# Compressed attention scores computed with the keys stationary and turned back by a stacked identity, and another order of products in attention's tail

## The chip, the cores and the metric

The kernel runs on one core of a Trainium2 chip. Times are device microseconds (us) of one execution. The kernel before took 708.16 us (median of 3 runs, 706.64 to 710.5). The change is judged by the same figure for the kernel after. The engines are named as in the profile: PE is TensorE (PEld its weight load), DVE VectorE, ACT ScalarE, POOL GpSimd, SP the queue that issues the weight loads.

## What is computed

A trunk of two equal layers over 256 tokens of width 1024. Each layer projects x, runs a short gated convolution on one half of the width and sparse attention (8 query heads in 2 key groups) on the other, normalises each head, projects back, adds and normalises; then comes a gated feed-forward part. The change touches one of attention's three branches, the compressed one, and what stands around it:

```python
sub = a.reshape(B, G, nsub, CMP_STRIDE, dk)
blocks = jnp.concatenate([sub[:, :, j:j + nc] for j in range(r)], axis=3)
k_cmp = gelu(blocks @ w1 + b1) @ w2 + b2          # nc = 15 compressed keys in each of 2 groups
sc = jnp.einsum('bgrqd,bgcd->bgrqc', qc, k_cmp)   # the compressed scores
p_cmp = _masked_softmax(sc, cmp_end[None, :] <= t[:, None])
o_cmp = jnp.einsum('bgrqc,bgcd->bgrqd', p_cmp, v_cmp)
out = g0 * o_cmp + g1 * o_slc + g2 * o_win
mixed = _head_rmsnorm(jnp.concatenate([conv_out, attn_out], -1), head_norm_g[i])
x = _layer_norm(ALPHA * x + mixed @ w_out[i], ln1_g[i], ln1_b[i])
```

## The kernel before

Everything is one program with the order on each engine written out by hand; the engines meet only at semaphores. The weights come through SP as units of 128x2048 numbers into three `raw` buffers. ACT rounds a unit to `ring_hi` (`split_hi`), DVE forms the remainder `ring_lo` (`split_lo`), and only then can the raw buffer be loaded again and PE use the unit. A precise product is three matmuls (`mm3`, L1194 to L1196): high by high, high by low, low by high. Plain float32 matmuls, such as those of L1279, L1345 and L1358, stand in the profile as two instructions each.

Attention is a loop over 12 blocks n = 0 to 11 (eight of 256 query-key columns for two heads, four of 128 columns for four heads). PE does, for each n: `scores(n+2)`, `transpose_p(n+1)` (L1266), some quarters of the convolution's projection (`conv_unit`), and `times_v(n)` (L1279). DVE takes the maxima and copies the transposed probabilities to `probsT` (L870); ACT takes the exponentials (`exps(n)`, L502). ACT works its list in order, and between `exps(n)` and `exps(n+1)` it does what the table `between` names: roundings of weights, parts of the convolution.

In the pass n = 10 PE also does, one after the other: the first product of the output projection (`out_part(L, 0, 0, 0)`, six matmuls of 512 columns, one mm3 for each half of the width), `mean_squares(L, 1)` (L1358: eight instructions of 2 columns), and `cmp_scores`, in which the queries are stationary and the 30 compressed keys `kcTh`, `kcTl` move: 2 token tiles by 4 head pairs by 3 matmuls, 24 matmuls of 30 columns. What follows is called the tail here: the last two `times_v`; `out_part(L, 0, 0, 1)`; `transpose_cmp` (L1336), which waits for the compressed softmax on DVE and ACT; `conv_roots(L, 1)` (L1368), which waits for a chain `copy_squares` (DVE L924), roots (POOL L704, L706), `roots_high` (ACT L510), `roots_low` (DVE L929); `times_v_cmp` for both token tiles (L1345); `out_part(L, 1, 0, 0)` and `(L, 1, 0, 1)`, which write banks 0 and 1; `out_unit(L, 0, 1)`; `heads_T(L, 0)` (L1388), six more matmuls, `heads_T(L, 1)`, and the rest of the output projection. Between `times_v_cmp` and `heads_T` lies a chain over three engines: DVE adds the compressed output (L910), ACT squares it, DVE sums (L915), POOL takes the root (L706), DVE scales (L920).

The first layer normalisation begins on DVE with `residual` (L952), after the splits of units 19 and 20, the first two of the feed-forward part.

## Time and profile before

| what | value |
|---|---|
| median of 3 runs | 708.16 us |
| the profiled execution | 708.14 us |
| its span, first to last instruction | 706.2 us |
| PE busy | 689.5 us, 98% |
| DVE busy | 519.5 us, 74% |
| ACT busy | 370.0 us, 52% |
| mean granted TensorE clock | 0.983 |

The profiled execution is the median one to 0.02 us, and 1.94 us of it lie outside its span. Busy time is no time at full speed: a matmul at half the clock is as busy as one at the full clock and takes up to twice as long. So for PE the row of the granted clock is read beside the busy share.

### The profile page before, as it was taken

To read this page: it belongs to the slowest core of one execution; us is meant where nothing else is said; L and a number is where in the kernel's file an instruction comes from. 1 tells how busy PE (TensorE), PEld (TensorE's weight loads), DVE (VectorE), ACT (ScalarE), POOL (GpSimd) and SP (SyncE) were. 2 spreads that over 40 slices of the span, in tenths; PEclk is the share of its full clock that TensorE was granted. 3 is DMA by queue.
4 is the path that set the end of the run, shared out by engine and by line. 5 is a ranking of instruction groups with operands and counts; after the bars stand their busy time and mean duration, and the time that the engine had idled before them with its cause. 6 is when DMAs were issued, how large, how long until landed. Compare 5 with 4: busy or idle time off the path is not lost.

```text
span 706.2 us, 11208 instructions
## 1 busy us (share of the span) xinstructions
PE 689.5 (98%) x4310; PEld 604.1 (86%) x4310; DVE 519.5 (74%) x762; ACT 370.0 (52%) x556; POOL 95.4 (14%) x54
## 2 busy tenths in 40 slices
PE   8999999999999999999999999999999999999995
PEld 5899998877998888888878999988889888888884
DVE  4675768768897777777696466697859977777756
ACT  5664535423776555666356443553248666666630
POOL 0000020221262111110000000204005511111000
PEclk9999999699999999999999999998999999999999
DMA  9971443332765555555338233513357855555301
GB/s 294 318 253 62 151 148 120 120 100 80 261 239 192 195 196 195 197 201 185 122 120 267 91 120 120 176 65 120 120 183 235 294 182 178 179 178 178 119 0 59
DMA packets 87401, 116.81 MB, mean 165 GB/s; under 512 B 5230, under 2 KB 73536, under 8 KB 87360
## 3 DMA queue, kind: packets, MB, share of 16 engines
q1 hardware_dynamic: 85920, 111.85, 47.6%
q10 hardware_dynamic: 1440, 4.39, 1.9%
q8 instruction: 28, 0.46, 0.3%
q14 instruction: 13, 0.11, 0.0%
HBM read 115.19 MB, written 1.05 MB: 165 GB/s over the span
## 4 chain that ended last, share of the span: by engine, by line
PE 92%; DVE 5%; DMA 1%; issue 1%; ACT 1%; SPq 0%; DVEq 0%; ACTq 0%
PE bank L1194 19%; PE bank L1196 18%; PE bank L1195 18%; PE bank L1454 17%; PE bank L1456 9%; PE bank L1279 3%; PE bank L1266 2%; DMA x_tok<-in_x 1%; PE bank L1215 1%; DVE x_tok L970 1%; DVE stats L954 1%; DVE x_tok L952 1%; PE bank L1258 1%; PE bank L1345 1%; DVE ring_lo L308 1%; DVE x_tok L978 1%
## 5 line engine op out<-in xcount | busy, mean ns | idle before, releaser
L308 DVE TENSOR_TENSOR ring_lo<-raw,ring_hi 128x2048 fp32r<-128x2048 f32 x102 | 232.6, 2285 | 23.0 <-ACT ring_hi L304 22.7
L304 ACT ACTIVATE ring_hi<-raw 128x2048 fp32r<-128x2048 f32 x102 | 194.3, 1908 | 13.2 <-DMA raw<-in_w_in 9.3
L1454 PE MATMUL bank<-xx,ring_hi 128*128 128x512 f32 x512 | 181.4, 398 | 0.0
L1456 PE MATMUL bank<-xx,ring_lo 128*128 128x256 f32 x512 | 143.8, 281 | 0.0
L1454 PEld LDWEIGHTS bank<-xx,ring_hi 128*128 128x128 f32 x512 | 96.2, 188 | 23.8
L1456 PEld LDWEIGHTS bank<-xx,ring_lo 128*128 128x128 f32 x512 | 96.7, 189 | 0.6
L721 POOL COPY step_par<-ffn_par 128x16 f32 (+1 forms) x22 | 64.3, 2927 | 221.5 <-DVE work L989 221.5
L1194 PE MATMUL bank<-xx,ring_hi 128*128 128x256 f32 x320 | 92.4, 289 | 0.0
L1195 PE MATMUL bank<-xx,ring_hi 128*128 128x256 f32 x320 | 90.5, 283 | 0.0
L1196 PE MATMUL bank<-xx,ring_lo 128*128 128x256 f32 x320 | 90.5, 283 | 0.0
L1194 PE MATMUL bank<-ring_hi,xx 128*128 128x512 f32 (+1 forms) x224 | 81.5, 364 | 3.8 <-DVE xx L783 3.8
L989 DVE SCALAR_TENSOR_TENSOR work<-conv_o,step_par,work 128x254 f32<-128x254 f32 (+1 forms) x128 | 56.2, 480 | 38.4 <-ACT work L560 37.2
L1194 PE MATMUL bank<-ring_hi,hTh 128*128 128x512 f32 (+1 forms) x224 | 81.0, 362 | 0.0
L1196 PE MATMUL bank<-ring_hi,hTl 128*128 128x512 f32 (+1 forms) x224 | 80.3, 358 | 0.0
L1195 PE MATMUL bank<-ring_lo,hTh 128*128 128x512 f32 (+1 forms) x224 | 80.1, 358 | 0.0
L1196 PE MATMUL bank<-ring_hi,xx 128*128 128x512 f32 (+1 forms) x224 | 78.1, 349 | 0.0
L1195 PE MATMUL bank<-ring_lo,xx 128*128 128x512 f32 (+1 forms) x224 | 77.9, 348 | 0.0
L556 ACT ACTIVATE conv_o<-bank 128x256 f32<-128x256 f32 x64 | 24.3, 379 | 74.1 <-PE bank L1456 74.1
L1194 PEld LDWEIGHTS bank<-xx,ring_hi 128*128 128x128 f32 x320 | 61.3, 192 | 0.2
L1195 PEld LDWEIGHTS bank<-xx,ring_hi 128*128 128x128 f32 x320 | 61.4, 192 | 0.0
L1196 PEld LDWEIGHTS bank<-xx,ring_lo 128*128 128x128 f32 x320 | 61.3, 192 | 0.0
L1194 PEld LDWEIGHTS bank<-ring_hi,xx 128*128 128x128 f32 x224 | 43.1, 192 | 11.2 <-DVE xx L783 3.8
(186 smaller groups left out, 998.1 us busy)
## 6 DMA issues: line engine op xcount, KB each, us to landing
raw<-in_w_up SPq DMA_DIRECT2D x44, 1024.0 KB, 5.2
raw<-in_w_down SPq DMA_DIRECT2D x22, 1024.0 KB, 5.0
raw<-in_w_in SPq DMA_DIRECT2D x21, 1024.0 KB, 5.2
raw<-in_cmp_w SPq DMA_DIRECT2D x8, 1024.0 KB, 5.9
raw<-in_w_out SPq DMA_DIRECT2D x8, 1024.0 KB, 4.8
qkv<-in_ln_g ACTq DMA_DIRECT2D x4, 512.0 KB, 3.6
qkv<-in_ln_b ACTq DMA_DIRECT2D x4, 512.0 KB, 5.0
raw<-in_w_in SPq DMA_DIRECT2D x2, 512.0 KB, 5.1
```

The costliest lines, as they stand in the source:

```text
L304: nc.scalar.activation(ring_hi[slot_of(L, u)][:], raw[raw_of(L, u)][:], ACT.Copy).then_inc(hi_done, 1)
L308: eng.tensor_tensor(ring_lo[slot_of(L, u)][:], raw[raw_of(L, u)][:], ring_hi[slot_of(L, u)][:].bitcast(fp32), ALU.subtract).then_inc(split ...
L556: nc.scalar.activation(up_y[:, 2 * v + c, :], bank[JOINED_BANK[2 * v + c]][:, SEQ:2 * SEQ], ACT.Copy).then_inc(up_low, 1)
L721: nc.gpsimd.tensor_copy(step_par[:, odd].rearrange("p v c k -> p (v c k)"), ffn_par[:, bass.ds(s, 1)].rearrange("p o v c k -> p (o v c k)"))\
L989: ins = V.scalar_tensor_tensor(ffn_y[:, odd, v, c, back:], up_source(s, odd, v, c)[:, 0:SEQ - back], step_par[:, odd, v, c, 2 - back:3 - b ...
L1194: pe.matmul(dst, ah, bh, start=start, stop=False, **kw)
L1195: pe.matmul(dst, ah, bl, start=False, stop=False, **kw)
L1196: return pe.matmul(dst, al, bh, start=False, stop=stop, **kw)
L1266: ins = pe.transpose(bank[6 + n % 2][:, P * m:P * (m + 1)], probs[n % 2][:, P * m:P * (m + 1)], ident)
L1279: ins = pe.matmul(bank[2][:, HEAD * (NPAIR * g + h):HEAD * (NPAIR * g + h + 1)], probsT[n % 2][:, P * (kb * j + b):P * (kb * j + b + 1)], ...
L1454: pe.matmul(dst[:], wh[:, k, P * c:P * (c + 1)], xx[:, k].rearrange("p a n -> p (a n)"), start=k == 0, stop=False)
L1456: ins = pe.matmul(dst[:, 0:SEQ], wl[:, k, P * c:P * (c + 1)], xh[:, k, :], start=False, stop=k == KT - 1)
```

## The change

The two key tiles become one, `kcT`, with high and low keys side by side (2 x 30 columns). `cmp_scores_wide(L, m)` makes them stationary and moves the queries of two head pairs, 2 x 256 columns, past them: one matmul gives 60 rows (high keys and low keys by high queries), a second adds high keys by low queries to the first 30 rows. It runs at the ends of the passes n = 4 and n = 6, into bank 3. ACT copies the 60 x 512 result to `cmp_sT` (`copy_wide`), once after `conv_init` behind `exps(5)`, once after `roots_high` behind `exps(7)`. In the pass n = 10 `cmp_scores` then only turns the result back: eight plain float32 matmuls with a 60 x 128 piece of `cmp_sT` stationary and an identity stacked twice (60 x 30, 30 more columns of the constants) moving, which also adds the two halves.

In the tail the order changes: the first product is divided around `mean_squares`, `out_part(L, 0, 0, 1)` moves ahead of `times_v(10)`, `conv_roots(L, 1)` and the two parts of token tile 1 move ahead of `transpose_cmp`, whose waits for the banks become weaker (the subtraction of the maxima instead of the exponentials). On DVE the split of unit 19 moves from before `copy_pT(11)` to between the two groups of `mix_low`.

```diff
+        kcT = sb("kcT", [P, 2, NG, NBLK], f32r)
+        kcTh, kcTl = kcT[:, 0], kcT[:, 1]
+        cmp_sT = sb("cmp_sT", [2 * NG * NBLK, 2, 2 * SEQ])
...
+            def copy_wide(L, m):
+                act.wait_ge(cmp_wide, 2 * L + m + 1)
+                nc.scalar.activation(cmp_sT[:, m, :], bank[3][0:2 * NG * NBLK, :], ACT.Copy).then_inc(cmp_wide_copied, 1)
...
-                           5: [lambda: conv_init(L, 1)], 6: [lambda: split_hi(act, L, 17)], 7: [lambda: roots_high(L, 0)],
+                           5: [lambda: conv_init(L, 1), lambda: copy_wide(L, 0)], 6: [lambda: split_hi(act, L, 17)],
+                           7: [lambda: roots_high(L, 0), lambda: copy_wide(L, 1)],
...
                 copy_squares(L, 1)
-                split_lo(V, L, 19)
                 copy_pT(L, 11)
...
                         mix_low(4 + j, xl[:, 4 + j, tok], xh[:, 4 + j, tok], bank[6 + t][:, P * j:P * (j + 1)])
-                split_lo(V, L, 20)
+                    split_lo(V, L, 19 + t)
...
+            def cmp_scores_wide(L, m):
+
+                if m == 0:
+                    pe.wait_ge(ms_read, 2 * L + 1)
+                    pe.wait_ge(cmp_copied, 2 * L + 2)
+                else:
+                    pe.wait_ge(cmp_wide_copied, 2 * L + 1)
+                n = NG * NBLK
+                heads = slice(2 * m, 2 * m + 2)
+                pe.matmul(bank[3][0:2 * n, :], kcT[:].rearrange("p a g c -> p (a g c)"),
+                          qTh[:, heads, :].rearrange("p i n -> p (i n)"), start=True, stop=False, skip_group_check=True)
+                pe.matmul(bank[3][0:n, :], kcTh.rearrange("p g c -> p (g c)"),
+                          qTl[:, heads, :].rearrange("p i n -> p (i n)"), start=False, stop=True,
+                          skip_group_check=True).then_inc(cmp_wide, 1)
+
             def cmp_scores(L):
...
-                        ins = mm3(bank[0][:, c0:c0 + NG * NBLK], qTh[:, h, tok], qTl[:, h, tok],
-                                  *(a[:].rearrange("p g c -> p (g c)") for a in (kcTh, kcTl)), True, True)
+                        col = SEQ * (h % 2) + P * t
+                        ins = pe.matmul(bank[0][:, c0:c0 + NG * NBLK], cmp_sT[:, h // 2, col:col + P],
+                                        cst[0:2 * NG * NBLK, C_ST:C_ST + NG * NBLK], start=True, stop=True)
...
                     elif n == 10:
                         pe.wait_ge(conv_out, 2 * L + 2)
-                        out_part(L, 0, 0, 0)
+                        wait_unit(L, U_OUT)
+                        wait_mix(L, 0, 0)
+                        out_product(L, 0, 0, 0)
                         mean_squares(L, 1)
+                        out_product(L, 0, 1, 0)
                         cmp_scores(L)
                     if n < 11:
                         transpose_p(L, n + 1)
+                    if n == 10:
+                        out_part(L, 0, 0, 1)
...
                     times_v(L, n)
-
-                out_part(L, 0, 0, 1)
+                    if n in (4, 6):
+                        cmp_scores_wide(L, (n - 4) // 2)
+
+                conv_roots(L, 1)
+                pe.wait_ge(exp_done, N_ATT * L + 12)
+                pe.wait_ge(max_done, N_ATT * L + 13)
+                out_part(L, 1, 0, 0)
+                out_part(L, 1, 0, 1)
                 transpose_cmp(L)
-                conv_roots(L, 1)
                 times_v_cmp(L, 0)
                 times_v_cmp(L, 1)
-                pe.wait_ge(exp_done, N_ATT * L + 13)
-                out_part(L, 1, 0, 0)
-                out_part(L, 1, 0, 1)
                 out_unit(L, 0, 1)
```

Three places in the order of instructions matter later. The first is ACT's list from `exps(5)` to `exps(8)`, the exponentials of four blocks with what lies between them. Before:

```order
L502 ACTIVATE probs,rsum<-bank,nmax 128x256 x2
L475 ACTIVATE conv_y<-conv_z,par 128x256 x2
L502 ACTIVATE probs,rsum<-bank,nmax 128x128 x4
L304 ACTIVATE ring_hi<-raw 128x2048
L502 ACTIVATE probs,rsum<-bank,nmax 128x128 x4
L510 ACTIVATE hTh<-croot 128x512
L502 ACTIVATE probs,rsum<-bank,nmax 128x256 x2
```

The same piece of the kernel after:

```order
L506 ACTIVATE probs,rsum<-bank,nmax 128x256 x2
L479 ACTIVATE conv_y<-conv_z,par 128x256 x2
L529 ACTIVATE cmp_sT<-bank 60x512
L506 ACTIVATE probs,rsum<-bank,nmax 128x128 x4
L308 ACTIVATE ring_hi<-raw 128x2048
L506 ACTIVATE probs,rsum<-bank,nmax 128x128 x4
L514 ACTIVATE hTh<-croot 128x512
L529 ACTIVATE cmp_sT<-bank 60x512
L506 ACTIVATE probs,rsum<-bank,nmax 128x256 x2
```

Each copy of a wide result now stands directly before the exponentials of a block, those of `exps(6)` and of `exps(8)`. The second place is PE at the end of the pass n = 4 of the kernel after, from `times_v(4)` to the first matmuls of `scores(7)`:

```order
L1287 MATMUL bank<-qkv,probsT 128x64 x4
L1337 MATMUL bank<-qTh,kcT 60x512
L1339 MATMUL bank<-qTl,kcT 30x512
L1202 MATMUL bank<-kTh,qTh 128x128
L1203 MATMUL bank<-kTl,qTh 128x128
L1204 MATMUL bank<-kTh,qTl 128x128
```

The two wide matmuls stand between `times_v(4)` and `scores(7)`, where nothing stood; at the end of the pass n = 6 it is the same with `scores(9)`. The third place is DVE's list from the scaling of the heads (`mroot`) to the first `residual`. Before, and then after:

```order
L920 TENSOR_TENSOR work<-work,mroot 128x512 x2
L938 SCALAR_TENSOR_TENSOR xx<-bank,par,xx 128x128 x8
L308 TENSOR_TENSOR ring_lo<-raw,ring_hi 128x2048
L952 SCALAR_TENSOR_TENSOR x_tok<-x_tok,bank 128x512
L954 BN_STATS stats<-x_tok 128x6
```

```order
L929 TENSOR_TENSOR work<-work,mroot 128x512 x2
L947 SCALAR_TENSOR_TENSOR xx<-bank,par,xx 128x128 x4
L312 TENSOR_TENSOR ring_lo<-raw,ring_hi 128x2048
L947 SCALAR_TENSOR_TENSOR xx<-bank,par,xx 128x128 x4
L312 TENSOR_TENSOR ring_lo<-raw,ring_hi 128x2048
L961 SCALAR_TENSOR_TENSOR x_tok<-x_tok,bank 128x512
```

A second split has moved in between the heads and the residual.

## Rows read from the trace of the kernel before

**Rows 1.** The page: granted TensorE clock in 40 slices of the span.

```profile
PEclk9999999699999999999999999998999999999999
```

**Rows 2.** Windows: stretch and length, busy us (instructions) of each engine, PEclk, DMA.

```profile
126.24:129.56 3.32, 3.32 (x31) 3.27 (x29) 3.31 (x3) 1.99 (x3) 1.12 (x1) 1.00 0.02 6
129.56:143.21 13.65, 13.65 (x46) 10.81 (x47) 8.57 (x22) 4.37 (x6) 2.70 (x2) 0.50 0.47 154
477.72:484.55 6.83, 6.83 (x29) 6.14 (x27) 5.97 (x18) 2.72 (x3) 1.97 (x2) 0.50 0.85 282
171.50:173.17 1.67, 0.00 (x0) 0.00 (x0) 0.75 (x2) 1.65 (x4) 0.00 (x0) 1.00 0.30 110
```

**Rows 3.** Timeline of PE, passes 4 to 7, layer 0: start, us, engine, line, operation.

```profile
105.33 1.00 PE L1279 MATMUL bank<-qkv,probsT 128*128 128x64 f32 x8
106.25 0.33 PE L1194 MATMUL bank<-kTh,qTh 64*128 64x128 f32 x1
...
107.96 0.60 PE L1266 MATMUL bank<-cst,probs 128*128 128x128 f32 x4
...
114.58 0.38 PE L1194 MATMUL bank<-kTh,qTh 64*128 64x256 f32 x1
...
115.74 0.66 PE L1266 MATMUL bank<-cst,probs 128*128 128x128 f32 x4
```

**Rows 4.** Timeline of ACT over the same passes.

```profile
89.60 0.60 ACT L468 ACTIVATE conv_z<-bank 128x512 f32<-128x512 f32 x1 [1.36 <-PE bank L1196]
...
104.58 0.37 ACT L502 ACTIVATE probs<-bank,nmax 128x128 f32<-128x128 f32 x1 [1.94 <-DVE nmax L862]
...
105.97 1.92 ACT L304 ACTIVATE ring_hi<-raw 128x2048 fp32r<-128x2048 f32 x1
...
114.67 0.47 ACT L502 ACTIVATE probs<-bank,nmax 128x256 f32<-128x256 f32 x1 [3.55 <-DVE nmax L862]
```

**Rows 5.** Timeline of layer 1 from the first output product to the compressed scores' end.

```profile
472.43 0.48 PE L1194 MATMUL bank<-ring_hi,xx 128*128 128x512 f32 x1
...
473.91 0.95 PE L1358 MATMUL bank<-cst,conv_sq 128*128 128x2 f32 x8
474.71 0.26 PE L1194 MATMUL bank<-kcTh,qTh 128*128 128x30 f32 x1
...
475.53 0.16 DVE L924 COPY cstat<-bank 128x8 f32<-128x8 f32 x1
...
477.39 0.87 PE L1266 MATMUL bank<-cst,probs 128*128 128x128 f32 x4
```

**Rows 6.** Timeline of DVE in layer 1's tail.

```profile
480.47 0.69 DVE L929 TENSOR_TENSOR hTl<-croot,hTh 128x512 fp32r<-128x512 f32 x1 [0.22 <-ACT hTh L510]
...
484.70 0.42 DVE L870 COPY probsT<-bank 120x256 f32<-120x256 f32 x1 [0.17 <-PE bank L1336]
...
490.91 0.69 DVE L920 TENSOR_TENSOR work<-work,mroot 128x512 f32<-128x512 f32 x1 [0.93 <-POOL mroot L706]
493.40 0.69 DVE L920 TENSOR_TENSOR work<-work,mroot 128x512 f32<-128x512 f32 x1 [1.80 <-POOL mroot L706]
...
497.24 2.28 DVE L308 TENSOR_TENSOR ring_lo<-raw,ring_hi 128x2048 fp32r<-128x2048 f32 x1
500.63 0.69 DVE L952 SCALAR_TENSOR_TENSOR x_tok<-x_tok,bank 128x512 f32<-128x512 f32 x1 [1.12 <-PE bank L1196]
```

**Rows 7.** Timeline of PE in layer 1's tail.

```profile
485.34 1.93 PE L1345 MATMUL bank<-stage,probsT 120*128 120x512 f32 x4
...
492.56 0.60 PE L1388 MATMUL bank<-cst,work 128*128 128x128 f32 x4
...
494.38 0.60 PE L1388 MATMUL bank<-cst,work 128*128 128x128 f32 x4
```

**Rows 8.** Timeline of PE in layer 0: first output product, and the second `heads_T`.

```profile
125.00 0.48 PE L1194 MATMUL bank<-ring_hi,xx 128*128 128x512 f32 x1
...
150.28 0.60 PE L1388 MATMUL bank<-cst,work 128*128 128x128 f32 x4
```

More of the change, by code:

```diff
@@ L64 @@
 C_MA, C_M01, C_BM, C_BLK = 320, 350, 380, 388
-C_ALL = C_BLK + 2
+C_ST = C_BLK + 2
+C_ALL = C_ST + NG * NBLK
 def shape_constants():
@@ L86, in shape_constants @@
     c[:, C_BLK:C_BLK + 2] = (p[:, None] // HEAD == np.arange(2)[None]) / HEAD
+    c[0:2 * NG * NBLK, C_ST:C_ST + NG * NBLK] = np.tile(np.eye(NG * NBLK), (2, 1))
     return c
@@ L195, in build @@
         hv = sb("hv", [P, 2, NH * NBLK])
-        kcTh = sb("kcTh", [P, NG, NBLK], f32r)
-        kcTl = sb("kcTl", [P, NG, NBLK], f32r)
+        kcT = sb("kcT", [P, 2, NG, NBLK], f32r)
+        kcTh, kcTl = kcT[:, 0], kcT[:, 1]
+        cmp_sT = sb("cmp_sT", [2 * NG * NBLK, 2, 2 * SEQ])
         vbd = stage[0:NH * NBLK, :].rearrange("p (h d) -> p h d", h=NH)
@@ L258, in build @@
         s_done, max_done, exp_done, cmp_p = sem("s_done"), sem("max_done"), sem("exp_done"), sem("cmp_p")
+        cmp_wide, cmp_wide_copied = sem("cmp_wide"), sem("cmp_wide_copied")
         pT_done, pT_copied, pv_done, o_read = sem("pT_done"), sem("pT_copied"), sem("pv_done"), sem("o_read")
@@ L1318, in cmp_v @@
                 pe.matmul(dst, ones[0:1, 0:NH * NBLK], b2[0:1, 1, :], start=False, stop=True).then_inc(cmp_done, 1)
+            def cmp_scores_wide(L, m):
[11 more added lines that the diff above has]
+                          skip_group_check=True).then_inc(cmp_wide, 1)
             def cmp_scores(L):
                 pe.wait_ge(exp_done, N_ATT * L + 11)
-                pe.wait_ge(cmp_copied, 2 * L + 1)
+                pe.wait_ge(cmp_wide_copied, 2 * L + 2)
                 for t in range(TT):
@@ L1326, in cmp_scores @@
                         c0 = NG * NBLK * (NPAIR * t + h)
-                        tok = slice(P * t, P * (t + 1))
-                        ins = mm3(bank[0][:, c0:c0 + NG * NBLK], qTh[:, h, tok], qTl[:, h, tok],
-                                  *(a[:].rearrange("p g c -> p (g c)") for a in (kcTh, kcTl)), True, True)
+                        col = SEQ * (h % 2) + P * t
+                        ins = pe.matmul(bank[0][:, c0:c0 + NG * NBLK], cmp_sT[:, h // 2, col:col + P],
+                                        cst[0:2 * NG * NBLK, C_ST:C_ST + NG * NBLK], start=True, stop=True)
                 ins.then_inc(s_done, 1)
@@ L1652, in _ @@
                     if n == 8:
+                        pe.wait_ge(cmp_wide_copied, 2 * L + 2)
                         conv_roots(L, 0)
                     times_v(L, n)
-                out_part(L, 0, 0, 1)
+                    if n in (4, 6):
[5 more added lines that the diff above has]
+                out_part(L, 1, 0, 1)
                 transpose_cmp(L)
-                conv_roots(L, 1)
                 times_v_cmp(L, 0)
                 times_v_cmp(L, 1)
-                pe.wait_ge(exp_done, N_ATT * L + 13)
-                out_part(L, 1, 0, 0)
-                out_part(L, 1, 0, 1)
                 out_unit(L, 0, 1)
```

## The prediction

> **What bounds the kernel now.** I read the table of busy time first, then the clock, then the tail by windows and timeline. PE is busy 98% of the span, so only what shortens PE's own work, or runs it at a faster clock, can gain. The clock row shows two dents, one in each layer's attention [rows 1]. The windows give them their size [rows 2]: in layer 0 the granted clock is 1.00 until 129.56 us and 0.50 for the next 13.65 us, in layer 1 it is 0.50 for 6.83 us. These are the two levels of 2.4 and 1.2 GHz. Before the first fall PE was not idle: it was busy for all 3.32 us of the window ahead of it, with the eight 2-column matmuls of `mean_squares` and most of the 30-column matmuls of `cmp_scores`. An idle PE, on the other hand, kept its clock: in 171.50 to 173.17 us it did nothing and 1.00 was granted. So the trace ties the dents to long runs of very thin matmuls, and these are what the change breaks up. At half the clock, work is paid twice: 20.48 us at 0.50 hold about 10.2 us that a full clock would save.
>
> The Trainium skill ("TensorE: Matmul & The Clock Gate", Why this matters for your kernels) puts a drop in the middle of a kernel down to idle gaps between bursts of matmuls. Here the measurement decides, and it shows a fall without an idle gap; by the page alone the dents would have another cause, and the change would leave them.
>
> **The change, step by step.** I use layer 1's times, and compare to the start of the first output product at 472.43 and to the second `heads_T` at 494.38, 21.95 us later [rows 5, 7]. In layer 0 the same distance is 150.28 - 125.00 = 25.28 us [rows 8], since its slow stretch was longer. Both layers run the same program there.
>
> *Work on PE at full clock.* From the first to the seventh matmul of 512 columns or what follows them takes 473.91 - 472.43 = 1.48 us, so three take 0.7 to 0.78 us. `mean_squares` takes 474.71 - 473.91 = 0.80 us, 0.10 us for each of eight instructions. The 24 thin score matmuls take 477.39 - 474.71 = 2.68 us [rows 5]. They go. In their place stand eight plain float32 matmuls, 16 instructions of 30 columns. No row shows a 60-row stationary of that kind; the nearest are 2 columns at 0.10 us and `times_v` with 64 columns at 0.92 / 8 = 0.115 us [rows 3]. So 1.6 to 1.84 us; I take 1.7. The turning back saves 1.0 us a layer.
>
> The skill (same page, LDWEIGHTS (loading the stationary operand)) says that the load of the stationary operand goes by its columns and not by its rows, so 60 rows would be no cheaper than 128. By it 128 columns take 107 ns, an estimate of 1.7 us for the 16.
>
> The wide matmuls add four of 512 columns a layer: 4 x 0.235 = 0.94 us (bounds 0.91 and 1.1, with three of 0.235 and one of 0.31 us as at a change of kind). So thin work is not saved in sum, it is made denser. If nothing ever waited, PE's path from the first product to the second `heads_T` would be 7.8 (products 3.04, `mean_squares` 0.8, turning back 1.7, four transposes 0.44, two `times_v` 1.84) + 0.87 (`conv_roots`, eight) + 2.8 (12 matmuls) + 0.22 (`transpose_cmp`) + 1.77 (`times_v_cmp`) + 2.73 (12 matmuls: 7.22 us between L1345 and L1388, less 1.77, halved, [rows 7]) + 1.82 (between the two `heads_T`) = 18.0 us. Transposes and `conv_roots` are taken at the 0.11 us of the thin matmuls (2.68 / 24), since all of them load 128 stationary columns. Against before that is -3.9 us in layer 1 and -7.3 in layer 0, with the wide matmuls -9.3 us in both together. This is what the change can give, with the clock at full throughout.
>
> *New waits, before the tail.* ACT works in order, so each wide copy holds up the exponentials behind it until PE has reached the wide matmuls. First copy, layer 0: `times_v(4)` ends at 106.25 [rows 3], the second wide matmul starts 0.24 us later and ends near 106.88, the copy takes 0.60 us like the copy of a bank at L468 [rows 4] and ends near 107.54. `exps(6)`, which now runs from 104.58 to about 106.05 and hence 1.5 us [rows 4], ends at 109.04. PE needs it for `transpose_p(6)`, at 107.96 now, 108.43 with 0.47 us of wide matmuls in front [rows 3]: it waits 0.65 us. Behind it on PE stand convolution and `times_v(5)`, all late by as much. Second copy: PE is late by 1.12 us, reaches the end of the second wide pair at about 116.33, the copy ends at 116.99, and `exps(8)` with its signal takes the 1.07 us between 114.67 and PE's start at 115.74 [rows 3, 4], so `transpose_p(8)` starts at 118.06. The shift has grown to 2.3 us a layer: 0.94 of work and 1.36 of waits. If the copies were free of this, 1.36 us a layer would fall away; if a copy takes 0.2 us more, 0.4 is added. PE's own later wait in the pass n = 9 hangs on a chain that starts from PE, and absorbs nothing.
>
> *New waits, in the tail* (start 474.73).
> - `conv_roots(1)` now stands after 7.8 us of work, at 482.5. Its chain took from 475.53 to 480.47 + 0.69 = 481.16, that is 5.63 us [rows 5, 6], and starts behind a split that is late by 2.3 too: ready at 483.5. Wait 0.95. In the old order it was covered by `transpose_cmp` and six slow products.
> - After it and 12 matmuls `transpose_cmp` starts at 487.2. The compressed softmax is ready by 485.2, since the roots on DVE are the last thing ahead of it. But the copy to `probsT` (0.42 us, [rows 6]) has nothing beside it now: transposes 0.5, copy 0.42, signals 0.1, less the 0.22 us counted as work: wait 0.8. `times_v_cmp` starts at 488.15.
> - From `times_v_cmp` to the end of the first scaling takes 490.91 + 0.69 - 485.34 = 6.26 us, to the end of the second 8.75 us [rows 6, 7]. Twenty-four matmuls covered this, now twelve do: PE is at `heads_T(0)` after 1.77 + 2.73 = 4.5 us and waits 1.8, and at `heads_T(1)` it waits 0.7, since POOL's second root is 2.49 us behind the first and PE has only 1.82 us between.
>
> Sum 4.2 us a layer. The second `heads_T` starts at 496.95: layer 1 loses 2.57 us. In layer 0 the same program gives 125.00 + 2.3 + 22.2 = 149.5 against 150.28: it gains 0.76.
>
> *The moved split.* It takes 2.28 us [rows 6] and frees DVE at `copy_pT(11)`, where the roots are the later condition anyway. Between the two groups of `mix_low` it uses up the 1.12 us that DVE waited for the output projection before `residual`. Counted from the second `heads_T`, residual was at +6.25 us; mix_low twice 1.1, two splits 2.28 each less overlap come to +6.5: +0.25 us a layer on a chain that PE waits for. The raw buffer of unit 19 comes free some 20 us later, and the load behind it on SP with it; unit 22 is used only after the first rows of the feed-forward part, about 15 us on, while its load takes 5.2 us. I cost it at nothing; if it were late, that would be up to 2 us. More constants are 15 KB in a load that is waited for much later: nothing.
>
> *Sum*: work -9.3, waits +2.7 (copies) and +8.4 (tail), splits +0.5: +2.3 us. Span 706.2 + 2.3 = 708.5, with the 1.94 us outside it **710.5 us**, 0.3% above the median of 708.16. A measurement of this kernel can tell about 0.5%, 704.6 or 711.7 us.
>
> **The rivals.**
> - *A, as summed* (chance 0.58): the clock holds and the waits take back what it gives; 708.5 to 712.5.
> - *B, slower: the clock falls again* (0.20). Place: from `mean_squares` through the turning back, 3.3 us with 0.8 us of dense work in the middle, or about the 0.95 us wait behind `times_v`. For it: 16 instructions of 30 columns remain thin. Against it: dense matmuls stand between the thin groups, and idle 1.67 us alone did not lower the clock [rows 2]. One fall of 6.83 us costs half of it, 3.4, less about 1 us of waits that it hides; in each layer one such gives 715, two long ones of 13.65 us near 720. It decides as soon as 1.2 us are lost. [...]
> - *C, the waits are about half as long* (0.14): a wide copy that ACT gets to earlier, or a shorter chain over POOL; 705 to 708.5, no change that can be told.
> - *D, faster: the waits are hidden* (0.08). If all 11.1 us of them were covered, 706.2 - 8.8 + 1.94 = 699; it decides when over half of them are, below 704.6. For it: each is a difference of long stretches. Against it: the two largest follow from rows without a choice.
>
> That the thin matmuls are not replaced is excluded by the order of instructions.
>
> **How the numbers follow.** The time is A's. C and A together reach from 705 to 712.5, B from 713 up. The range 706 to 716 leaves out D (0.08), a piece of C (0.02) and half of B (0.10). Faster is D, 0.08. Slower is B and the top of A above 711.7 (0.12 of it): 0.32. The rest, 0.60, is the same.
>
> **What would show it.** In the profile after: granted clock 1.00 in both tails (A) or a dent (B); PE idle before `transpose_p(6)` and `transpose_p(8)` behind ACT's exponentials, 0.65 us each or so; idle before `conv_roots(1)`, before `times_v_cmp` and before both `heads_T`, 4.2 us a layer; layer 0's tail a little shorter, layer 1's about 2.6 us longer. The prediction is wrong if the clock falls, if the idle time in attention is under half of 5.5 us a layer, or if unit 22 is late.

## The result and the profile after

The kernel after takes 710.93 us (median of 17 executions, 707.49 to 714.31), the kernel before 707.44 us (17 executions beside them, 704.16 to 713.97). The ratio is 1.0048, 95% interval 1.0028 to 1.0068: slower by half a per cent, a small difference, but the interval leaves out 1. The prediction was 710.5 us with 706 to 716. Ratios, here and below, leave out executions more than 1.5% above the fastest of their kernel (one each in e1, e2, e3 and e8, two in e6).

Three lines of the page of the kernel after (busy time, PE in 40 slices, granted clock in 40 slices):

```profile
PE 682.2 (97%) x4302; PEld 594.4 (84%) x4302; DVE 518.7 (73%) x762; ACT 371.7 (53%) x560; POOL 91.4 (13%) x54
...
PE   8999999988999999999999999998999999999995
...
PEclk9999999999999999999999999999999999999999
```

Both dents of [rows 1] are gone, and PE's row has 8s where they were (layer 1) or just behind (layer 0), where PE waits now. But this execution is not a typical one. It took 707.49 us (span 705.7), the shortest of the 17, and its mean clock was 0.998; the others had 0.987 to 0.996. So the profile shows what the program costs when the clock holds, and the median also holds what the clock costs. Both are needed below.

PE in the passes n = 4 to 8 of layer 0, to be read beside [rows 3]:

```profile
106.07 0.42 PE L1337 MATMUL bank<-qTh,kcT 128*60 128x512 f32 x1
106.33 0.40 PE L1339 MATMUL bank<-qTl,kcT 128*30 128x512 f32 x1
...
108.79 0.66 PE L1274 MATMUL bank<-cst,probs 128*128 128x128 f32 x4 [0.26 <-ACT probs L506]
...
115.35 0.42 PE L1337 MATMUL bank<-qTh,kcT 128*60 128x512 f32 x1
115.61 0.40 PE L1339 MATMUL bank<-qTl,kcT 128*30 128x512 f32 x1
...
117.59 0.66 PE L1274 MATMUL bank<-cst,probs 128*128 128x128 f32 x4 [0.47 <-ACT probs L506]
```

`transpose_p(6)` moved from 107.96 to 108.79 and `transpose_p(8)` from 115.74 to 117.59. This trace runs 0.08 us early at that place (`times_v(4)` ends by so much sooner), so the shift is 0.91 and then 1.93 us. Before, neither of the two had a wait. The waits in the shift are 0.26 + 0.47 = 0.73 us; each wide pair takes 0.59 us until PE is at the next product (106.66 and 115.94). ACT shows why PE waits, as said in the prediction: the copy L529 stands ahead of the exponentials.

```profile
106.76 0.59 ACT L529 ACTIVATE cmp_sT<-bank 60x512 f32<-60x512 f32 x1 [4.19 <-PE bank L1339]
107.26 0.35 ACT L506 ACTIVATE probs<-bank,nmax 128x128 f32<-128x128 f32 x1
...
116.04 0.59 ACT L529 ACTIVATE cmp_sT<-bank 60x512 f32<-60x512 f32 x1 [3.61 <-PE bank L1339]
116.54 0.46 ACT L506 ACTIVATE probs<-bank,nmax 128x256 f32<-128x256 f32 x1
```

PE in the tail of layer 0 (start, busy time, what it waited for), the counterpart of [rows 8]; layer 1 shows the same distances:

```profile
126.86 0.48 PE L1202 MATMUL bank<-ring_hi,xx 128*128 128x512 f32 x1
...
127.64 0.95 PE L1381 MATMUL bank<-cst,conv_sq 128*128 128x2 f32 x8
...
129.33 1.97 PE L1351 MATMUL bank<-cst,cmp_sT 60*128 60x30 f32 x16
131.22 0.66 PE L1274 MATMUL bank<-cst,probs 128*128 128x128 f32 x4
...
134.80 0.30 PE L1391 MATMUL bank<-ident_r,hTh 128*128 128x128 f32 x1
...
138.55 0.38 PE L1359 MATMUL bank<-cst,probs 128*120 128x128 f32 x2
139.45 1.98 PE L1368 MATMUL bank<-stage,probsT 120*128 120x512 f32 x4 [0.52 <-DVE probsT L879]
...
143.29 0.47 PE L1202 MATMUL bank<-ring_hi,xx 128*128 128x512 f32 x1 [1.86 <-DVE xx L947]
...
146.14 0.60 PE L1411 MATMUL bank<-cst,work 128*128 128x128 f32 x4
...
148.31 0.66 PE L1411 MATMUL bank<-cst,work 128*128 128x128 f32 x4 [0.17 <-DVE work L929]
```

The turning back takes 131.22 - 129.33 = 1.89 us. `conv_roots(1)` at 134.80 waits for nothing. `times_v_cmp` waits 0.52 us, the output unit behind it 1.86, the second `heads_T` (L1411) 0.17. From the first product to the second `heads_T` it is 148.31 - 126.86 = 21.45 us, and in layer 1 it is 493.80 - 472.35 = 21.45 again.

PE's waits over the whole span (us in total, times, longest) give the same as a sum; these rows have grown or are new (before, PE waited for the exponentials 1.3 us in all, twice 0.6, and for none of the others):

```profile
PE bank L1202 <- DVE xx L947: 3.7, 2, 1.9
PE bank L1274 <- ACT probs L506: 2.7, 6, 0.6
...
PE bank L1368 <- DVE probsT L879: 1.0, 2, 0.5
PE bank L1411 <- DVE work L929: 0.4, 2, 0.2
```

### The profile page after: what moved, and what is told of

It reads as the page before. It is cut to its first block, busy times and chain, and to the rows that moved or that the text cites. A ratio compares the mean times of both kernels' runs of the same rounds, so it can differ in the third digit from the quotient of the medians.

```text
span 705.7 us, 11200 instructions
## 1 busy us (share of the span) xinstructions
PE 682.2 (97%) x4302; PEld 594.4 (84%) x4302; DVE 518.7 (73%) x762; ACT 371.7 (53%) x560; POOL 91.4 (13%) x54
## 4 chain that ended last, share of the span: by engine, by line
PE 86%; DVE 8%; issue 1%; ACT 1%; DMA 1%; POOL 1%; SPq 0%; DVEq 0%; ACTq 0%; POOLq 0%
PE bank L1202 17%; PE bank L1477 17%; PE bank L1204 16%; PE bank L1203 16%; PE bank L1479 9%; PE bank L1287 3%; DVE ring_lo L312 2%; PE bank L1274 2%; DMA x_tok<-in_x 1%; DVE x_tok L979 1%; DVE stats L963 1%; PE bank L1223 1%; DVE x_tok L961 1%; ACT probs L506 1%; DVE x_tok L987 1%
## 5 line engine op out<-in xcount | busy, mean ns | idle before, releaser
L1202 PE MATMUL bank<-ring_hi,xx 128*128 128x512 f32 (+1 forms) x224 | 79.6, 355 | 7.5 <-DVE xx L792 3.8
L1204 PE MATMUL bank<-ring_hi,xx 128*128 128x512 f32 (+1 forms) x224 | 77.2, 345 | 0.0
```

Source lines behind the costliest of these rows:

```text
L1202: pe.matmul(dst, ah, bh, start=start, stop=False, **kw)
L1204: return pe.matmul(dst, al, bh, start=False, stop=stop, **kw)
```

## The experiments

**How the runs are compared.** Executions of one kernel differ by up to 10 us, and nearly all of it goes with the mean granted clock. For each execution the time at half the clock is 2 x (1 - mean clock) x span, less 2.4 us for the very end of the span, where PE has no work and the clock is down in every profile. (In the profiled executions this last stretch is 2.8 to 6.2 us long, so a single figure can be up to 4 us too high, for time that costs nothing.) A straight line through the spans over these times has a slope of 0.30 to 0.45 us per us and leaves 0.4 to 1.1 us. Its value at zero is called the fitted span at full clock below. It is an extrapolation: for the kernel before, whose clock never rose above 0.992, a long one. "Ratio" is against the kernel before on the same chip. The last two columns take every execution; in brackets stands what they become without those that the ratio leaves out.

| kernel | median us | ratio (95%) | fitted span at full clock | mean us at half clock |
|---|---|---|---|---|
| before (four sets) | 706.6 to 708.1 | | 697.7 to 698.5 | 18.6 to 21.3 |
| after | 710.93 | 1.0048 (1.0028 to 1.0068) | 705.5 | 9.3 |
| e1 before again | 707.46 | 0.9980 (0.9961 to 1.0) | 698.0 (697.8) | 20.2 (18.8) |
| e2 after again | 712.40 | 1.0075 (1.0047 to 1.0104) | 705.0 (705.2) | 16.2 (12.7) |
| e3 copies behind | 710.75 | 1.0049 (1.0028 to 1.0071) | 702.6 (702.4) | 15.8 (14.2) |
| e4 filler | 707.79 | 1.0017 (0.9989 to 1.0045) | 701.3 | 16.0 |
| e5 wide only | 709.19 | 1.0029 (1.0 to 1.0057) | 701.7 | 17.8 |
| e6 tail only | 711.84 | 1.0032 (0.9996 to 1.0067) | 703.0 (702.9) | 16.8 (13.6) |
| e7 split back | 713.28 | 1.0088 (1.0058 to 1.0118) | 706.3 | 13.6 |
| e8 early transposes | 703.38 | 0.9949 (0.9923 to 0.9975) | 699.9 (700.2) | 7.6 (5.8) |
| e9 few thin | 706.18 | 0.9985 (0.9958 to 1.0012) | 698.4 | 15.9 |
| e10 thin, early transposes | 706.71 | 1.0009 (0.9987 to 1.0031) | 699.7 | 12.8 |
| e11 e8 again | 705.40 | 0.9983 (0.9956 to 1.0011) | 699.9 | 11.2 |
| e12 dense instead | 707.81 | 0.9996 (0.9977 to 1.0014) | 702.7 | 10.3 |

The standard error of the fitted span is 0.3 to 0.8 us (1.0 for e2 in brackets), and 1.6 us for e9, whose executions lie close together in clock. That of the mean time at half clock is 0.8 to 2.8 us, and 3.9 us for the six executions of e2, so that only differences of several us say something.

**e1 and e2: both kernels once more, unchanged.**

> The kernel before, unchanged, to see span and granted clock of many executions side by side. Theory: the times spread because the granted clock does, so mean clock and time go together; from the profiled execution (0.983, 706.2 us) I expect clocks of 0.975 to 0.99 and about 0.4 us of span more for each us at half clock. Rival: the spread has another source (DMA), and clock and time are not tied.

> The kernel after, unchanged. Its profiled execution was the fastest of 17 (707.49 us, clock 0.998, no stretch at half clock outside the end); the others had 0.987 to 0.996. Theory: the clock still falls in most executions, for 3.4 to 14 us, in attention, and that is the 3.4 us between that execution and the median of 710.93; this profile should show a dent in a tail, starting within a few us of mean_squares and the 30-column matmuls or at the waits behind them. Rival: the slower executions differ by something else, and a profile at 710 us has no dent.

The kernel before repeats itself. The kernel after does as a program (705.0 against 705.5 us at full clock). Its time at half clock, 16.2 (12.7) us instead of 9.3, is not clear of the spread of six executions. The profiled execution of e2 has falls where that of the kernel after had none, as expected. PE where the clock fell in layer 0, and windows of 2 us in layer 0 and layer 1 (busy time of each engine, then the granted clock, DMA share, GB/s):

```profile
143.38 0.70 PE L1202 MATMUL bank<-ring_hi,xx 128*128 128x512 f32 x1 [1.86 <-DVE xx L947]
```

```profile
142.00:144.00 2.00, 0.62 (x2) 0.55 (x3) 2.00 (x5) 0.68 (x2) 0.88 (x2) 0.86 0.00 0
144.00:146.00 2.00, 2.00 (x6) 1.53 (x5) 0.92 (x2) 0.00 (x0) 1.83 (x3) 0.50 0.03 8
146.00:148.00 2.00, 2.00 (x9) 1.57 (x8) 0.35 (x1) 0.00 (x0) 2.00 (x3) 0.78 0.00 0
478.00:480.00 2.00, 2.00 (x9) 1.84 (x9) 0.52 (x1) 0.63 (x1) 1.19 (x1) 0.50 0.89 259
```

One fall (3.41 us) follows the wait of 1.86 us, the other (3.41 us) begins at 477.96 us, in the turning back, which runs from 476.28 to 478.33 with `mean_squares` and three dense matmuls ahead of it. The second is a place that the prediction named for its rival B. The first is not: B named the wait behind `times_v`, and this one is the wait behind `times_v_cmp`.

**e3: both copies behind exponentials that are already due.** The first `copy_wide` moves from pass 5 to pass 6, the second from 7 to 8.

```
-  5: [lambda: conv_init(L, 1), lambda: copy_wide(L, 0)], 6: [lambda: split_hi(act, L, 17)],
-  7: [lambda: roots_high(L, 0), lambda: copy_wide(L, 1)],
-  8: [lambda: split_hi(act, L, 18)],
+  5: [lambda: conv_init(L, 1)], 6: [lambda: copy_wide(L, 0), lambda: split_hi(act, L, 17)],
+  7: [lambda: roots_high(L, 0)],
+  8: [lambda: copy_wide(L, 1), lambda: split_hi(act, L, 18)],
```

> The kernel after with each wide copy moved behind the exponentials that it stands before (first behind exps(6), second behind exps(8)). Theory: PE's waits for exps(6) and exps(8) in front of transpose_p(6) and (8), 0.4 and 0.5 us a layer in the profiled execution, go: 0.9 to 1.2 us a layer, 1.8 to 2.4 us in all against the kernel after, at equal clock. Rival: those waits would only move to the pass n = 9, where PE waits 0.6 us for exps(10), or to split_hi(18): below 0.5 us in all.

The fitted span falls by 2.9 us against the kernel after and by 2.4 against e2, which ran beside it. PE's waits for L506 fall from 2.7 to 1.2 us (1.2 in e8 too, which has the same edit), as much as the kernels without a wide copy have (1.3 in e6 and e12). So the wait behind the copies is real and a matter of one position in ACT's queue: 0.75 us a layer by PE's waits, 0.98 by the start of the first product (125.88 in e8, below, instead of 126.86), and up to 1.4 by the fit. Beside e2, with about the same time at half clock, the median is 1.65 us lower (710.75 and 712.40); against the kernel after, which had less time at half clock, it hardly moved.

**e4: four dense matmuls among the thin scores of the kernel before**, so that no long thin run is left; bfloat16, 512 columns, into an unused bank.

```
+                pe.wait_ge(pT_copied, N_ATT * L + 10)
...
+                        if h % 2 == 0:
+                            pe.matmul(bank[7][:], warm[:, 0:P], warm[:], start=True, stop=True)
```

> The kernel before with four more matmuls of 512 columns (bf16 ones, result not used) spread among the 24 thin score matmuls, nothing else changed. They add 4 x 0.21 = 0.85 us of PE work a layer. Theory: the long run of thin matmuls is what brings the clock down, so the dents vanish or become rare: clock 0.99 or more, and a time below the kernel before by 10.2 us of half-clock loss less 1.7 us of filler less 2 to 5 us of waits for the compressed softmax and the heads that the slow clock hid: 703 to 706 us. Rival: the clock falls for another reason (the transposes, times_v, the waits); then the clock stays near 0.983 and the time rises by 1.7 us.

Half-clock time goes from 21.3 (the kernel before beside it) to 16.0 us, far from zero, and the median does not move: the theory missed its 703 to 706 us. The thin run is not all of it.

**e5 and e6: the two halves of the change by themselves.** e5 has the wide scores and the turning back and leaves order and splits of the tail as they were; e6 has the new order and the moved split with the thin scores.

> The kernel before with the wide scores alone (wide matmuls, ACT copies, turning back), the old order in the tail and on DVE. Times of several executions are compared at the same clock: fitted on its 29 executions beside the last runs, the kernel before has a span of 697.7 us at full clock, the kernel after 705.5. Theory: the wide scores cost 0.94 us of matmuls and 1.0 us of waits for the copies a layer and give back 0.8 us of thin work: about 700 at full clock. If instead the wide scores carry the whole loss, 705; if they are free, 698. Clock: less time at half clock than before (21 us by the mean clock) if the long thin run matters, the same if not.

> The kernel before with the new order in the tail and the moved split alone, the 24 thin score matmuls kept. Theory: most of the loss at full clock is here, since 12 matmuls no longer cover the chain from times_v_cmp to the heads (PE waited 1.86 us a layer for mix_conv_low and 0.5 for the copy of probsT): 703 at full clock, against 697.7 before. Rival: the waits in the tail are the same in the old order once the clock is full, since the chain over DVE, ACT and POOL is the bound in both: then 698 to 699.

The ratios are 1.0029 and 1.0032, and 1.0048 (e2: 1.0075) for both halves together: neither is a gain that the other spoils, though each of the two intervals reaches 1.0, so that the shares of the two can't be told. The fitted span of e6, 703.0 as expected, whose clock reached 0.996, is a short extrapolation; that of e5 (up to 0.989) is as long as that of before, and is not compared further.

**e7: the splits put back where they were**, the rest as after.

```
+                split_lo(V, L, 19)
...
-                    split_lo(V, L, 19 + t)
+                split_lo(V, L, 20)
```

> The kernel after with split_lo of unit 19 put back before copy_pT(11). In the kernel before POOL's first small instruction of the roots took 2.16 us while that split ran on DVE, in the kernel after 0.20 us with DVE idle. Theory: POOL waits for the split, which reads two tiles of SBUF; so here it takes 2.1 us or more again, roots_low comes about 1.9 us later and PE waits 0.9 us for it ahead of conv_roots: 1.5 to 2 us more than the kernel after at the same clock, at most 0.3 us won back at the residual. Rival: the 2.16 us have another cause (the first use after a long idle); then POOL takes 0.2 us and the time is the same as after.

This answers why `conv_roots(1)` did not wait in the kernel after. POOL's two instructions on the second roots in the kernel before, in the kernel after, and in e7, in this order:

```profile
128.44 2.16 POOL L704 TENSOR_SCALAR cstat<-cstat 128x8 f32<-128x8 f32 x1 [28.64 <-DVE cstat L924]
130.69 1.65 POOL L706 TENSOR_TENSOR croot<-cstat,neg_half 128x8 f32<-128x8 f32 x1
```

```profile
130.31 0.20 POOL L713 TENSOR_SCALAR cstat<-cstat 128x8 f32<-128x8 f32 x1 [30.58 <-DVE cstat L933]
130.59 1.65 POOL L715 TENSOR_TENSOR croot<-cstat,neg_half 128x8 f32<-128x8 f32 x1
```

```profile
130.43 2.17 POOL L713 TENSOR_SCALAR cstat<-cstat 128x8 f32<-128x8 f32 x1 [30.57 <-DVE cstat L933]
132.68 1.66 POOL L715 TENSOR_TENSOR croot<-cstat,neg_half 128x8 f32<-128x8 f32 x1
```

And what DVE did beside it in the kernel before, and PE's wait in e7:

```profile
128.26 2.29 DVE L308 TENSOR_TENSOR ring_lo<-raw,ring_hi 128x2048 fp32r<-128x2048 f32 x1
```

```profile
135.78 0.33 PE L1392 MATMUL bank<-ident_r,hTh 128*128 128x128 f32 x1 [0.66 <-DVE hTl L938]
```

An operation of 0.20 us takes 2.16 us when the split of a weight block runs on DVE, and 0.20 when it doesn't. It ends at 130.60, right behind the split's end at 130.55: it is held up rather than slowed. The rival, a first use after a long idle, is out, since the idle time before it is as long in all three.

The chain that `conv_roots(1)` waits for, in the kernel after, from its first operation on DVE to its last:

```profile
129.95 0.16 DVE L933 COPY cstat<-bank 128x8 f32<-128x8 f32 x1
...
133.78 0.68 DVE L938 TENSOR_TENSOR hTl<-croot,hTh 128x512 fp32r<-128x512 f32 x1
```

With the split back, the wait before `conv_roots` is there (0.66 us), the tail takes 22.32 instead of 21.45 us in both layers, and the profiled execution (clock 0.997, no fall) has a span of 707.3 instead of 705.7 us; the fitted spans, 706.3 and 705.5, differ by half as much, within their errors. The moved split, costed at +0.25 us a layer, is worth about -0.8. The Trainium skill states this ("SBUF — State Buffer", SBUF: two separate sides, and Who interferes with whom): an operation of VectorE with two inputs in SBUF holds a port pair that it shares with GpSimd, and GpSimd stands still meanwhile. The split is such an operation, and by that rule the trace agrees.

**e8, e10, e11: the transposes of the compressed probabilities ahead of the first output group**, so that their copy to `probsT` and the first `times_v_cmp` have work beside them. e8 is e3 with this; e10 is e6 with this (thin scores); e11 is e8 once more beside e10.

```
                 conv_roots(L, 1)
+                transpose_cmp(L)
                 pe.wait_ge(exp_done, N_ATT * L + 12)
                 pe.wait_ge(max_done, N_ATT * L + 13)
                 out_part(L, 1, 0, 0)
-                out_part(L, 1, 0, 1)
-                transpose_cmp(L)
                 times_v_cmp(L, 0)
                 times_v_cmp(L, 1)
+                out_part(L, 1, 0, 1)
```

> The kernel with the copies behind the exponentials, and in the tail transpose_cmp directly behind conv_roots, one part of token tile 1 between it and times_v_cmp, the other behind. Theory: times_v_cmp starts 1.15 us earlier a layer (138.3 instead of 139.45 us in the trace of after) and six matmuls more cover the chain behind it: 2.3 us less than with the copies behind alone (702.6 at full clock), so 700.3, and a median about equal to the kernel before, 707 to 708.5. Rival: the chain behind times_v_cmp does not follow; then 702 to 703 at full clock.

> Scores thin as in the kernel before, splits and products as in the kernel after, and transpose_cmp moved ahead of the first output group as in e8. It is e8 without the wide scores, and e6 with the early transposes. The early transposes should again take 2.7 to 3 us off the fitted span at full clock: 703.0 becomes about 700.2. If the wide scores are what keeps the clock up, the mean time at half clock stays near e6's 16.8 us, against e8's 7.6 us, and the median is about 700.2 + 0.41 x 16.8 + 1.9 = 709 us. Rival: e8's quiet clock came with its shorter waits and not with the wide scores; then about 8 us at half clock here too, and about 705.5 us.

> e8 once more, beside e9 and e10 on one chip: is it faster than the kernel before on a second occasion? If so, the median is 703 to 705 us and the ratio 0.992 to 0.998, with 5 to 11 us at half clock. If its quiet clock was the state of that chip at that time, 12 to 16 us at half clock and 705.5 to 708 us.

PE in the tail of layer 0 in e8:

```profile
125.88 0.48 PE L1202 MATMUL bank<-ring_hi,xx 128*128 128x512 f32 x1
...
135.13 0.43 PE L1359 MATMUL bank<-cst,probs 128*120 128x128 f32 x2 [0.23 <-DVE probs L1136]
...
137.23 1.98 PE L1368 MATMUL bank<-stage,probsT 120*128 120x512 f32 x4 [0.27 <-DVE probsT L879]
...
141.07 0.47 PE L1202 MATMUL bank<-ring_hi,xx 128*128 128x512 f32 x1 [0.47 <-DVE xx L947]
...
146.09 0.66 PE L1411 MATMUL bank<-cst,work 128*128 128x128 f32 x4 [0.20 <-DVE work L929]
```

The wait of 1.86 us is down to 0.47, and first product to second `heads_T` takes 20.21 us instead of 21.45. All three have fitted spans of 699.7 to 699.9 us, about 3 below their base as expected. e8 beat the kernel before (0.9949), where 707 to 708.5 us had been expected; its repetition is level (0.9983, interval 0.9956 to 1.0011). The program repeats (699.9 twice); its time at half clock was 7.6 (5.8) and then 11.2 us, a difference of the size of its error. e10, with thin scores, has 12.8 us beside e11's 11.2 on the same chip; it lies between its two forecasts (16.8 and 8). So the quiet clock of these kernels cannot be put down to the wide scores.

**e9 and e12: is it the thin matmuls that lower the clock?** Both leave out seven eighths of the compressed scores (21 of the 24 thin matmuls a layer). e9 puts nothing in their place, e12 puts ten dense matmuls there that take as long (the first three lines added below are e12's alone).

```
-                for t in range(TT):
-                    for h in range(NPAIR):
+                pe.wait_ge(pT_copied, N_ATT * L + 10)
+                for _ in range(10):
+                    pe.matmul(bank[7][:], warm[:, 0:P], warm[:], start=True, stop=True)
+                for t in range(1):
+                    for h in range(1):
```

> The kernel before with three of the 24 thin compressed-score matmuls a layer (one of eight pairs of block and head pair), so it leaves out seven eighths of the compressed scores and the rest of its attention reads what stands in the bank. PE has 21 x 0.112 = 2.35 us less work a layer: the fitted span at full clock should go from 698.1 to about 693.4. Theory (the run of thin matmuls is the main cause of the falls): the mean time at half clock goes from 20 us to 5 us or less, median about 693.4 + 0.4 x 5 + 1.9 = 697.3 us. Rival (the falls come from something else, and the thin run only stands near them): 15 to 20 us at half clock stay, median about 702 to 703.3 us.

> As e9 (seven eighths of the compressed scores left out), but ten bfloat16 matmuls of 512 columns into an unused bank stand where the 21 thin ones were: 10 x 0.235 = 2.35 us against 21 x 0.112 = 2.35 us. So neither the path nor the waits change against the kernel before, and only the thinness goes. The fitted span at full clock should stay at 698 us. Theory (the thin run is the main cause of the falls): 5 us or less at half clock, median near 698 + 0.4 x 5 + 1.9 = 702 us. Rival (thin matmuls are no cause): 17 to 20 us at half clock, as in the kernel before, and a median of 706.5 to 708 us.

In e9 the theory missed and the rival was right on the clock: it stays low for 15.9 us, against 18.6 beside it. Both missed the span (698.4 and not 693.4): 2.35 us less work a layer brings nothing, since PE now waits up to 2.1 us for `copy_pT(11)`, which used to be covered. PE's row and windows of 5 us in e9:

```profile
131.38 1.97 PE L1279 MATMUL bank<-qkv,probsT 128*128 128x64 f32 x8 [2.10 <-DVE probsT L870]
```

```profile
125.00:130.00 5.00, 4.28 (x33) 3.88 (x31) 4.95 (x6) 2.82 (x5) 1.39 (x1) 1.00 0.05 10
130.00:135.00 5.00, 3.62 (x13) 3.23 (x14) 4.19 (x12) 2.45 (x3) 2.44 (x2) 0.50 1.08 358
```

The clock falls to 0.50 here at 130.04 us, 0.76 us into PE's idle 2.10 us (129.28 to 131.38). Ahead of that PE was busy, with `mean_squares`, three of the 24 thin score matmuls, transposes and `times_v`. e12 halves the time at half clock (10.3 us against 20.9 of the kernel before beside it), with PE's order kept and its length to within 0.3 us a layer. That is the cleanest test, and it missed both its forecasts (5 us or less, 17 to 20): dense work in this place takes away about half of the time at half clock, and no more. Leaving the thin matmuls out with a wait in their stead (e9) takes away little. So it is not shown that thinness by itself is the cause; a wait there did nearly the same. e12's trace shows something more important. PE in the tail of layer 0 in e12, where no clock fell:

```profile
125.06 0.48 PE L1194 MATMUL bank<-ring_hi,xx 128*128 128x512 f32 x1
...
127.56 2.10 PE L1326 MATMUL bank<-warm 128*128 128x512 bf16 x9
129.31 0.37 PE L1194 MATMUL bank<-kcTh,qTh 128*128 128x30 f32 x1
...
135.46 0.44 PE L1339 MATMUL bank<-cst,probs 128*120 128x128 f32 x2 [1.64 <-DVE probs L1128]
...
137.56 1.98 PE L1348 MATMUL bank<-stage,probsT 120*128 120x512 f32 x4 [0.82 <-DVE probsT L870]
...
146.68 0.60 PE L1391 MATMUL bank<-cst,work 128*128 128x128 f32 x4
```

And the same distance in its layer 1, with a window from its fall of the clock (0.50 from 479.95 to 486.75, 6.80 us):

```profile
468.78 0.48 PE L1194 MATMUL bank<-ring_hi,xx 128*128 128x512 f32 x1
...
493.05 0.60 PE L1391 MATMUL bank<-cst,work 128*128 128x128 f32 x4
```

```profile
480.00:485.00 5.00, 4.48 (x9) 2.23 (x9) 2.46 (x5) 1.53 (x3) 0.00 (x0) 0.50 0.00 0
```

Layer 0 is the old order at full clock: it waits 1.64 us for the compressed softmax and 0.82 us for the copy, waits that no row of before shows, because slow products filled them. The tail takes 146.68 - 125.06 = 21.62 us, against 25.28 in layer 0 of before and 21.95 in layer 1 [rows 5, 7, 8]. So the kernel before at an undisturbed clock would have a span of 706.2 - 3.66 - 0.33 = 702.2 us (an estimate from these traces), near e12's fitted span (702.7), and not the 698 that its own line extrapolates to. Its own fastest executions agree: with 9 to 13 us at half clock they have spans of 702.3 to 702.9, so the first ten us cost next to nothing, and the line is too steep there. e5, the old order with the wide scores, has 21.62 us in its layer 0 too.

## Why the prediction held, and where it did not

- **The time.** 710.5 predicted, 710.93 measured, inside the range and in the case that was given 0.60 (within 0.5%) by a hair. That it lies so close is luck. Two errors cancel: the span at full clock came out 2.8 us lower than the sum (705.7 against 708.5), and the clock did not hold, as A had assumed, in most executions. The profiled one is A; the median is 3.4 us above it, by rival B, which had 0.20. One of the prediction's own signs of being wrong, a falling clock, came true in e2's profile and, by the mean clocks, in most of the 17. The other two did not: PE's new waits are 0.73 + 2.55 = 3.28 us a layer, over half of 5.5, and it never waits for unit 22.
- **What a full clock gives back.** "20.48 us at 0.50 hold about 10.2 us that a full clock would save" is about PE's own work; the time gains less. By e12 the order before gains 3.66 + 0.33 = 4.0 us. The 6.83 us at half clock in layer 1 cost only 0.33 us, since they lay on stalls; in layer 1 of e12 a fall of the same length behind the stalls cost 24.27 - 21.62 = 2.65 us. The prediction did not go wrong by this, because it charged the uncovered waits one by one, and so arrived at a tail of 22.2 us with a full clock.
- **What lowers the clock.** "The trace ties the dents to long runs of very thin matmuls" is the step of the argument that was too strong. Dense work in place of the thin run took away about half of the half-clock time (e12), a wait in its place hardly any (e9). The clock fell also without a long thin run: 0.76 us into a wait of 2.10 us (e9), and right behind one of 1.86 us (e2), which the idle 1.67 us of [rows 2] had seemed to exclude. A wait alone doesn't decide it either: the kernel after waited 1.86 us without a fall. The Trainium skill's rule on idle gaps ("TensorE: Matmul & The Clock Gate", Why this matters for your kernels), which the prediction set aside for the row, speaks of longer gaps than any of these. The only such gap in these runs is the end of the span, where the clock falls 2.0 (e4) to 5.3 us (after) behind PE's last matmul; there the traces agree. The fall in [rows 2], with PE busy for 3.32 us ahead of it, does not agree.
- **Turning back.** 1.89 us instead of 1.7. The bound (1.6 to 1.84) was short by 0.05; 16 instructions at 0.118 us.
- **Wide matmuls.** 1.18 us a layer (two pairs of 0.59) instead of 0.94, above the bound of 1.1: PE loses 0.1 us more at the change back to the scores' 64-row operands. (Three of 0.235 and one of 0.31, as the bound was worked out, make 1.02; one change of kind for each pair makes 1.1.)
- **Copy waits.** Place and mechanism right, 0.26 + 0.47 = 0.73 us a layer instead of 1.36. At the first, `exps(6)` began at 107.26, 0.2 us sooner than reckoned (0.50 us behind the copy's start, and not at its end), and PE came 0.2 us later than reckoned. Both shorten the wait, 0.65 - 0.4. Their sum with the wide matmuls, 1.93 us, is nearer to the 2.3 predicted.
- **Tail waits.** 0.52 + 1.86 + 0.17 = 2.55 us a layer against 4.2. `conv_roots` 0 instead of 0.95 is the term that failed. Its chain took 4.51 us (DVE's copy at 129.95 to the end of `roots_low` at 134.46) and not 5.63. POOL's small operation was 1.96 us shorter, since the split no longer stood beside it; 0.84 us of this went again, as `roots_low` now stood behind DVE's work on the compressed softmax. The moved split, costed at +0.25, caused it (e7, where the chain takes 5.65 us and the wait is back). Before `times_v_cmp` 0.52 instead of 0.8. The large wait was sized right (1.8, measured 1.86) but stands one step sooner, at the first output unit behind `times_v_cmp`, which needs `mix_conv_low(1)` (L947), and that stands in DVE's list behind the sums of the same chain; the 0.7 at the second `heads_T` shrank to 0.17, since PE now comes to it later (argued from the rows).
- **The path without waits.** 21.45 - 2.55 = 18.9 us a layer instead of 18.0: turning back 0.2, the rest small gaps where one kind of matmul follows another (argued from the rows, not tested). This took back half of what the waits gave.
- **Residual.** +6.33 us behind the second `heads_T` instead of +6.24: 0.1 and not 0.25 a layer. Unit 22 was not late.
- **The balance at full clock.** A layer: 1.93 us of shift ahead of the tail, less 21.62 - 21.45 = 0.17 in it, 1.76; twice this is 3.5 us, the 702.2 to 705.7 of the spans. So the change as a program loses: it trades 0.8 us of thin work (2.68 for 1.89) for 1.18 of wide work and 0.73 of waiting behind a copy, and its new order has as many waits as the old. It has less time at half clock, 9 to 16 us instead of 19 to 21, but that is worth nothing in the median: by the same estimate the slow stretches cost the kernel before 707.44 - 1.94 - 702.2 = 3.3 us, since they lay on waits, and the kernel after 710.93 - 707.49 = 3.4 us.

**What stays open.** What lowers the clock is only half answered. Executions of one kernel differ by 10 us and more in their time at half clock, and what differs between them is not in any row. Some falls have neither a thin run nor a wait ahead of them that others lack: e1 has one at 469.9 us for 20.48 us, before the tail of layer 1 begins, in a wait of 0.64 us that every one of these kernels has there. Whether the shorter waits or something else quieted e8, e10 and e11 was not separated.

## What to carry to other kernels

A slow stretch of the clock is not worth half its length: run the same order once at full clock (here by filling in dense work of equal length) and read the waits that open, before counting on the difference. When an operation is moved, look at what it stood beside on the other engines, and not only at its own queue: the split's neighbour on POOL was worth more (0.87 us) than the split's own place (0.1). A copy that is put in an in-order engine's queue belongs behind the work that is due sooner, and a transpose whose result takes a chain of steps belongs as early as its input allows: these two moves gave 5.6 us at full clock (705.5 to 699.9), and e8 is 2.3 us below the 702.2 estimated for the kernel before.

## What the runs showed of the hardware

- A POOL operation on 128x8 numbers took 2.16 us instead of 0.20 beside a 128x2048 DVE operation with two SBUF inputs, in before and e7, where the split ran, and 0.20 us in after, where it didn't.
- The granted clock fell to 0.50 with PE busy for the 3.32 us ahead of it (before), and 0.76 us into an idle stretch of 2.10 us without a long thin run (e9). In e12 it stayed at 1.00 through waits of 1.64 and 0.82 us in layer 0, and in layer 1 it fell 0.8 us behind the same first wait (1.61 us). Executions of the kernel before on one chip had mean clocks from 0.974 to 0.989 beside e12.
- Between executions of one kernel, one us more at half clock went with 0.30 to 0.45 us more span (the lines of the table above). Single stretches cost from 0.05 us each (6.83 us in layer 1 of before) to 0.39 (6.80 us in layer 1 of e12), by what they cover.
- A plain float32 matmul with 60 rows and 30 columns stands as two instructions of 0.118 us each (after), no cheaper than the thin score matmuls with 128 rows (2.68 / 24 = 0.112 us, before).
